# Normalizing by token halves at four stage borders of a two-block transformer kernel, with one gate product a tile moved from conv_out to gqa_out

## What is computed

```
def _modulate(t, g, shift, scale):
    return _rms(t, g) * (1 + scale) + shift
...
def _swiglu(h, w13, w2):
    gte, up = jnp.split(h @ w13, 2, axis=-1)
    return (jax.nn.silu(gte) * up) @ w2
...
        lat = lat + 0.5 * mod[:, 0, 2] * _swiglu(_modulate(lat, norm_g[i, 0], mod[:, 0, 0], mod[:, 0, 1]), ffn_w13[i, 0], ffn_w2[i, 0])
        if cx is not None:
            cx = cx + 0.5 * modc[0, 2] * _swiglu(_modulate(cx, norm_g[i, 0], modc[0, 0], modc[0, 1]), ffn_w13[i, 0], ffn_w2[i, 0])
        h = _modulate(lat, norm_g[i, 1], mod[:, 1, 0], mod[:, 1, 1])
...
        lat = lat + mod[:, 1, 2] * y
```

## Time and profile before

| | us |
|---|---|
| median of three runs | 2092.98 |
| lowest and highest of them | 2090.76 and 2093.58 |
| the profiled execution | 2093.39 |
| its span, first to last instruction | 2091.6 |

### The profile page before, as it was taken

How to read it: one execution, slowest core, us unless ns; L and a number is a source line. 1 busy time by engine, 2 the same in 40 slices (tenths; PEclk the granted TensorE clock), 3 DMA queues, 4 the chain that set the end, 5 groups by cost and what they waited for, 6 DMA issues and landing times.

```text
span 2091.6 us, 26725 instructions
## 1 busy us (share of the span) xinstructions
PE 1908.9 (91%) x10092; PEld 1624.7 (78%) x10092; DVE 1402.9 (67%) x2091; ACT 683.9 (33%) x910; POOL 126.5 (6%) x78
## 2 busy tenths in 40 slices
PE   2973799789999998998999999989999998889998
PEld 2952788778888887886788888878888887678998
DVE  7868799986666676668766666676666225856554
ACT  2443356432222213332322222232222223444432
POOL 2001300200000010002000001100000010010000
PEclk9975799889999999999999999999999999999999
DMA  9840955423443443334333344434333323223444
GB/s 377 313 168 3 238 206 188 181 93 149 150 150 125 167 175 124 134 148 151 121 143 133 146 149 159 164 121 151 141 134 118 105 94 122 91 81 141 162 163 158
DMA packets 75737, 315.77 MB, mean 151 GB/s; under 512 B 19060, under 2 KB 22904, under 8 KB 56344
## 3 DMA queue, kind: packets, MB, share of 16 engines
q1 hardware_dynamic: 75136, 314.15, 41.9%
q10 hardware_dynamic: 536, 0.79, 0.1%
HBM read 313.86 MB, written 1.06 MB: 151 GB/s over the span
## 4 chain that ended last, share of the span: by engine, by line
PE 74%; DVE 18%; ACT 3%; issue 2%; DMA 1%; POOL 1%; SPq 0%; DVEq 0%; ACTq 0%
PE acc L1294 72%; DVE Wl L810 4%; ACT Wh L526 2%; DVE tmp L797 2%; PE psN L1294 1%; DVE psGT L842 1%; DVE psGT L839 1%; DVE psGT L845 1%; DVE najunk L845 1%; DVE najunk L842 1%; DVE XT L797 1%; DMA afirst<-in_ada_w 1%; DVE small L967 1%; PE psN L1356 1%; DVE tmp L985 1%
## 5 line engine op out<-in xcount | busy, mean ns | idle before, releaser
L1294 PE MATMUL acc<-Hh,Wh 128*128 128x512 f32 (+1 forms) x2320 | 809.0, 349 | 57.1 <-DVE Hl L797 23.4
L1294 PE MATMUL acc<-Hl,Wh 128*128 128x512 f32 (+1 forms) x2320 | 801.1, 345 | 0.0
L1294 PE MATMUL acc<-Hh,Wl 128*128 128x512 f32 (+1 forms) x2320 | 800.4, 345 | 0.0
L810 DVE TENSOR_TENSOR Wl<-raw,Wh 128x2048 fp32r<-128x2048 f32 (+1 forms) x214 | 449.6, 2101 | 273.0 <-ACT Wh L526 273.0
L1294 PEld LDWEIGHTS acc<-Hh,Wh 128*128 128x128 f32 x2320 | 448.5, 193 | 119.3 <-issue 62.2
L526 ACT ACTIVATE Wh<-raw 128x2048 fp32r<-128x2048 f32 (+1 forms) x214 | 374.3, 1749 | 352.0 <-PE acc L1294 336.7
L1294 PEld LDWEIGHTS acc<-Hl,Wh 128*128 128x128 f32 x2320 | 448.7, 193 | 50.6 <-issue 0.7
L1294 PEld LDWEIGHTS acc<-Hh,Wl 128*128 128x128 f32 x2320 | 448.1, 193 | 50.7
L1294 PE MATMUL acc<-hidh,Wh 128*128 128x512 f32 (+1 forms) x704 | 259.0, 368 | 0.9 <-DVE Wl L810 0.9
L1294 PE MATMUL acc<-hidl,Wh 128*128 128x512 f32 (+1 forms) x704 | 258.6, 367 | 0.0
L1294 PE MATMUL acc<-hidh,Wl 128*128 128x512 f32 (+1 forms) x704 | 258.6, 367 | 0.0
(11 more groups left out here) (222 smaller groups left out, 1193.8 us busy)
## 6 DMA issues: line engine op xcount, KB each, us to landing
raw<-in_ffn_up SPq DMA_DIRECT2D x88, 1024.0 KB, 4.7
graw<-in_mod_w SPq DMA_DIRECT2D x144, 512.0 KB, 5.4
raw<-in_ffn_down SPq DMA_DIRECT2D x64, 704.0 KB, 4.0
graw<-in_ada_w SPq DMA_DIRECT2D x32, 512.0 KB, 6.2
raw<-in_odd_in SPq DMA_DIRECT2D x16, 1024.0 KB, 4.9
raw<-in_even_in SPq DMA_DIRECT2D x12, 1024.0 KB, 6.8
raw<-in_conv_in SPq DMA_DIRECT2D x12, 1024.0 KB, 4.7
afirst<-in_ada_w SPq DMA_DIRECT2D x8, 1024.0 KB, 13.1
```

What stands on the lines that cost most here:

```text
L810: nc.vector.tensor_tensor(Wl[:, half, 0:f], raw[:, slot, 0:f], Wh[:, half, 0:f].bitcast(f32), ALU.subtract)\
L1294: return nc.tensor.matmul(out, lhsT, rhs, start=start, stop=stop)
```

## The change

Four borders are treated by token halves: those into conv_in, ffn1_up, ffn2_up and gqa_kv (`HALVED`). At the end of the old stage the last output (the last pair of ffn_down tiles, or the last conv_out tile with its two blocks, `LAST`) is computed first for the 256 latent tokens, then for the 256 context tokens, in matmuls of 256 columns. TensorE's latent sums and the spread of the latent factors stand inside or behind the context half (`last_halved`, `lat_sums`, `lat_spreads`). The next stage begins with the latent half of its tiles 0 and 1, then the context half of both (`first_two_halved`); the context sums and spread stand behind blocks 3 and 7 of the first latent half and go to the bank psT[1], the latent ones to psN. For gqa_kv it is the latent half of the key tile, the two latent blocks of the value tile, the context half of the keys, the two context blocks of the values. VectorE does all of it in `halves_norm`, ScalarE in the new branches of `splits` and `norm`; the split of the next stage's second tile stands on both between the latent blocks and the context blocks. New semaphores lat_* carry the latent half; the context half keeps the old ones, and drained["dve"] counts one less in each of the three ffn_down stages ahead of such a border. Beside this, four tiles of gate products move from conv_out (two a tile to one) to gqa_out (none to one). The diff, cut to its core (in order: the table of stages; ScalarE's norm; VectorE's halves_norm; TensorE's first two tiles, last conv_out tile, last ffn_down pair; its program):

```diff
-    ("conv_out", 4, 16, 0, TOK, 2, "dve"),
+    ("conv_out", 4, 16, 0, TOK, 1, "dve"),
...
-    ("gqa_out", 4, 16, 0, LAT, 0, "dve"),
+    ("gqa_out", 4, 16, 0, LAT, 1, "dve"),
...
+        if name in ("ffn0_down", "ffn1_down", "ffn2_down"):
+            drained[by] -= 1
...
+        HALVED = {n: i for i, n in enumerate(["conv_in", "ffn1_up", "ffn2_up", "gqa_kv"])}
+        LAST = {n: (KC - 2, KC - 1) if n == "ffn1_up" else (KC - 1,) for n in HALVED}
...
+                if name in HALVED:
+                    for k in range(KC):
+                        act.wait_ge(lat_t, KC * HALVED[name] + k + 1)
+                        nc.scalar.activation(Hh[:, k, CL], tmp[:, k % 2, CL], ACT.Identity, bias=affine(name, k, 0)[1])\
+                            .then_inc(lat_hi, 1)
+                        if k == 2:
+                            act.wait_ge(drained["dve"], S[X_FROM[name]].drained1)
+                            for q in LAST[name]:
+                                square_half(name, q, CC)
+                    split(S[name].n0 + 1, early=True)
+                    for k in range(KC):
+                        act.wait_ge(n_t, KC * i + k + 1)
+                        nc.scalar.activation(Hh[:, k, CC], tmp[:, k % 2, CC], ACT.Identity, bias=affine(name, k, 1)[1])\
+                            .then_inc(n_hi, 1)
+                    return
...
+                dve.wait_ge(lat_done, l + 1)
+                residual_half(0, CL).then_inc(lat_res, 1)
+                meanwhile()
+                mean(0, psN, lat_ss, l + 1).then_inc(lat_mean, 1)
+                if not ffn:
+                    split(S[name].n0)
+                dve.wait_ge(lat_spread, l + 1)
+                scaled(0, 0, CL, psN).then_inc(lat_t, 1)
+                if ffn:
+                    split(S[name].n0)
+                for k in range(KC):
+                    if k + 1 < KC:
+                        if k > 0:
+                            dve.wait_ge(lat_ready, KC * l + k)
+                        scaled(k + 1, 0, CL, psN).then_inc(lat_t, 1)
+                    dve.wait_ge(lat_hi, KC * l + k + 1)
+                    low(k, 0, CL).then_inc(lat_ready, 1)
+                    if k == 2:
+                        dve.wait_ge(tile_done, s.n0 + s.tiles)
+                        residual_half(1, CC).then_inc(drained["dve"], 1)
+                    if k == 6:
+                        mean(1, psT[1], n_ss, i + 1).then_inc(n_mean, 1)
+                split(S[name].n0 + 1, early=True)
+                dve.wait_ge(n_spread, i + 1)
+                scaled(0, 1, CC, psT[1]).then_inc(n_t, 1)
+                for k in range(KC):
+                    if k + 1 < KC:
+                        if k > 0:
+                            dve.wait_ge(h_ready, H0[name] + k)
+                        scaled(k + 1, 1, CC, psT[1]).then_inc(n_t, 1)
+                    dve.wait_ge(n_hi, KC * i + k + 1)
+                    low(k, 1, CC).then_inc(h_ready, 1)
...
+                pe.wait_ge(lo_ready, s.n0 + 1)
+                pe.wait_ge(drained[s.by], s.drained0)
+                part(0, CL, lat_ready, KC * l, {3: ctx_sums, 7: ctx_spread})
+                pe.wait_ge(lo_ready, s.n0 + 2)
+                pe.wait_ge(drained["dve"], prev.drained1)
+                part(1, CL, lat_ready, KC * l, {})
+                part(0, CC, h_ready, H0[name], {}).then_inc(tile_done, 1)
+                part(1, CC, h_ready, H0[name], {}).then_inc(tile_done, 1)
...
+                    if halved(s) and isinstance(t, int) and t == s.tiles - 1:
+                        sum_of_sums(X_TO[s.name])
+                        for h, hc in enumerate((CL, CC)):
+                            for j in range(2):
+                                for k in range(KC):
+                                    last = three(acc[u % 2][h][:, j * LAT:(j + 1) * LAT], u % 2, j * KC + k, xh[:, k, hc], xl[:, k, hc],
+                                                 k == 0, k == KC - 1)
+                                if h == 1 and j == 0:
+                                    lat_sums(X_TO[s.name])
+                            last.then_inc((lat_done, tile_done)[h], 1)
+                        lat_spreads(X_TO[s.name])
+                        return
...
+                    part(0, 0, CL)
+                    sum_of_sums(name)
+                    part(0, 1, CL).then_inc(lat_done, 1)
+                    part(1, 0, CC, lat_sums).then_inc(tile_done, 1)
+                    lat_spreads(name)
+                    part(1, 1, CC).then_inc(tile_done, 1)
...
             ffn_down(S["ffn0_down"])
-            norm("conv_in")
             linear(S["conv_in"])
             linear(S["conv_out"], xh=cyh, xl=cyl)
-            norm("ffn1_up")
             linear(S["ffn1_up"])
```

More of the change, by code:

```diff
@@ L212, in build @@
         c_tanh = sem("c_tanh")
+        lat_done, lat_res, lat_sq, lat_ss, lat_mean, lat_rstd, lat_spread, lat_t, lat_hi, lat_ready = (
+            sem("lat_" + x) for x in ("done", "res", "sq", "ss", "mean", "rstd", "spread", "t", "hi", "ready"))
         nmx = small[:, 0:64]
@@ L905, in step @@
                 def step(t, u, i):
+                    if halved(s) and t == s.tiles - 1:
+                        modulation_of(s, t, u, i)
+                        return
                     next_split(s, t, u, i)
@@ new lines, in ctx_sums, with ctx_spread @@
+            def ctx_sums(name):
+                pe.wait_ge(n_sq, KC * NORMS[name] + KC)
+                for q in LAST[name]:
+                    for b in range(2):
+                        ins = nc.tensor.matmul(psT[1][:, b:b + 1], tmp[:, q % 2, (2 + b) * P:(3 + b) * P], ones[:, 0:1],
+                                               start=False, stop=q == KC - 1, skip_group_check=True)
+                ins.then_inc(n_ss, 1)
+            def ctx_spread(name):
+                pe.wait_ge(n_rstd, NORMS[name] + 1)
+                for b in range(2):
+                    ins = spread(psT[1][:, b * P:(b + 1) * P], rstd, 2 + b)
+                ins.then_inc(n_spread, 1)
@@ L1361, in sum_of_sums @@
                 pe.wait_ge(n_sum, SUM0[name] + SUMMED[name])
+                if name in HALVED:
+                    for h, bank in enumerate((psN, psT[1])):
+                        for b in range(2):
+                            nc.tensor.matmul(bank[:, b:b + 1], tmp[:, 2, (2 * h + b) * P:(2 * h + b + 1) * P], ones[:, 0:1],
+                                             start=b == 0, stop=False, skip_group_check=True)
+                    return
                 sum_of(name, tmp[:, 2, :], True, False)
```

117 lines of the change are left out of this document (108 added, 9 removed).

## The result

The changed kernel takes **2099.42 us** (median of 9 runs, 2097.94 to 2101.36), the kernel before 2093.24 (median of 9, 2090.76 to 2094.44): a ratio of 1.0032, with a 95% interval of 1.0024 to 1.0040. It is 6 us slower. The prediction was 2096.0, range 2089 to 2103: the time is in the range, but above the bound of 2097.2 under which I had called it no change, so the outcome is one to which I had given 0.37. The profiled execution took 2101.36, 8.0 above that of before.

The account below looks back on a forecast made before the run. TensorE is busy 91% of the span; winnable is its idle or low-clock time at stage borders. -2.3 - 0.9 - 2.4 + 5.2 + 3.5 = +3.1 on 2093.39 gives 2096.5, as median 2096.0, range 2089 to 2103.

Parts of the forecast that it names:

- The border into conv_in: Into conv_in: with halves and a high clock, tile 1 done at 823.8 instead of 826.1, a gain of 2.3 us.
- Four stands of the sum: At conv_in, TensorE waits: 0.5 before the sum of sums, 1.1 before block 0, 0.9 for the context residual, 2.5 before tile 1.
- rival (a): Clock also falls in short stands at conv_in, gqa_kv, ffn2_up: 2.4 us each, +7, 2103; chance 0.20.
- ffn2_up and gqa_kv: Borders into these stages: gain 0.9 us at ffn2_up (2.3 less 1.4), gain 2.4 at gqa_kv (2.3 + 0.7 less 0.6).
- The border into ffn1_up: From conv_out: TensorE stands 7.2 us before the last tile, the clock falls; a loss of 5.2 us.
- My bound for a clock that holds: At the border from conv_out into ffn1_up: the loss is 2.1 us if the clock stays up.
- gqa_out: In gqa_out: added product pairs and slower GpSimd adds make the last residual 3.5 us late, a loss of 3.5.
- the 5.5 us at half clock: Behind the old border into conv_in: matmuls ran 5.5 us at 1.2 GHz, counted as a cost.
- (b): At conv_out: TensorE is not held at the sum of sums, all borders gain as designed, 2088 to 2085; chance 0.07.
- (c): Clock held at conv_out (2.1) and the products at gqa_out swallowed, 2089.5; chance 0.10.
- (d): Splitting matmuls into 256 columns costs almost nothing, 2091.4, a border gain of 1 to 1.5 each; chance 0.08.
- my 13: Splitting a 512-column matmul into two of 256 columns costs 13 ns a pair, from 0.120 against 0.227 us.

Follow-up runs that it names:

- before again: The kernel before, unchanged, profiled a second time; 2094.04 us.
- products_only: The kernel before with only the table of stages changed: one pair of gate products a tile in conv_out and in gqa_out; 2091.87 us, ratio 0.9997.
- products_ffn2: The kernel before with four of conv_out's eight pairs of gate products moved into ffn2_down's first four tiles, none in gqa_out; 2088.50 us, ratio 0.9983.
- halves_and_ffn2: The changed kernel with the sum of sums directly ahead of the latent sums, and four product pairs in ffn2_down's first tiles, none in gqa_out; 2086.02 us, ratio 0.9966.
- experiment 4: The run conv_out_busy: the changed kernel with 25 unread matmuls in the stand before the last conv_out tile; 2095.86 us, ratio 1.0016.
- conv_out_busy: The changed kernel with 25 matmuls nobody reads put into TensorE's stand before the last conv_out tile; 2095.86 us, ratio 1.0016.
- three_borders: The changed kernel with ffn1_up's border and the gate products as before, halves only into conv_in, ffn2_up and gqa_kv; 2091.47 us, ratio 0.9992.
- products_back: The changed kernel with the gate products back: two pairs a tile in conv_out, none in gqa_out; 2097.88 us, ratio 1.0024.
- before_kept_busy: The kernel before with unread matmuls in the three stands of each norm; 2092.23 us, ratio 0.9997.
- halves_kept_busy2: halves_and_ffn2 with unread matmuls filling TensorE's stands at the borders, the fewer-matmul version in ffn3_up's norm; 2083.45 us, ratio 0.9955.
- sum_late: The changed kernel with the sum of sums moved from the head of the last conv_out tile to directly ahead of the latent sums; 2089.47 us, ratio 0.9984.

## Why the prediction was right or wrong, step by step

**The border into conv_in: steps right, clock wrong.** Four stands of the sum were met within 0.12 us, and tile 1 was done at 824.2 against a forecast of 823.8. The profile of the changed kernel shows the gain of 2.3 (2.5), but it is the rarer case: in its second profile, and in six of seven with this border halved and its stand empty, the clock fell behind the stand of 2.4 us, and 1.0 is left. That is rival (a). It names the right mechanism at a price of 2.4 where 1.5 was measured here and at gqa_kv, and the fall comes and goes from one execution to the next, which neither the forecast nor the rival had as a possibility.

**ffn2_up and gqa_kv.** 0.8 and 0.2 against a forecast of 0.9 for ffn2_up, and 1.4 and 2.9 against 2.4 for gqa_kv. But other profiles of the kernel before (before again, products_only, products_ffn2) are themselves 0.9 to 1.0 faster at gqa_kv than the one I measured against; against those the halves bring 0.5 or 2.0.

At ffn2_up the sum held that lost time is free for TensorE as long as it would only wait for tile 1's weights. The runs bear this out, for the clock too. Tile 1's first matmul in halves_and_ffn2, where the clock stays up, and in the changed kernel, where it is at half from 1371.6 on; then the second profile of the changed kernel, where the half clock lasts longer:

```profile
1370.22 0.39 PE L1411 MATMUL acc<-Hh,Wh 128*128 128x256 f32 x1 [1.69 <-DVE Wl L865]
...
1379.32 0.38 PE L1410 MATMUL acc<-Hh,Wh 128*128 128x256 f32 x1 [0.21 <-DVE Wl L864]
...
1370.20:1376.60 6.40, 5.34 (x26) 5.37 (x26) 4.46 (x11) 3.93 (x7) 0.00 (x0) 0.50 0.55 225
```

The wait shrinks from 1.69 to 0.21 us and the column is -0.8 in both. With the longer stretch no wait is left before tile 1 and the gain is 0.2. So a fall costs 0 to 0.6 us here, where rival (a) had 2.4.

**The border into ffn1_up: right, 5.0 and 4.4 against 5.2.** The stand before the last tile (6.3 for 7.2), its releaser, the clock's fall in it and the 4.29 before ffn1_up (in the sum: 4.7 from the stage's end to the first matmul) are as described. Inside the sum the clock was too small: 3.4 and not 2.7 (experiment 4), the stand itself too large. My bound for a clock that holds, 2.1, does not follow from my own terms (5.2 less 2.7 and 1.0 is 1.5). Experiment 4 lost 1.6, but there the clock fell once more behind the last tile, so no run tests this bound as such.

**gqa_out: the products right, what stands around them left out.** The last residual came 3.4 late (20.66 less 17.27) against 3.5; products_only, with the same products, lost 3.4 in all. (The pair is 2.8 us by its own rows, 788.53 to 791.33, and not 2.7.) But the end of the kernel is 4.8 and 5.0 late. The sum was closed at the last residual, and the traces show what it left out:

- A fall of the clock at the end of the attention delays the first residual of gqa_out as well, by 0.5 and 0.7 us in the two profiles. Of the thirteen profiles against the first of before, the six with such a fall lose 0.1 to 0.7 there, the seven without lose nothing.
- From the last residual to the first matmul of ffn3_up it takes 7.4 us in each kernel whose stands are empty. But the half clock behind the last residual reaches a different way into the first tile of ffn3_up. Its 48 matmuls take 7.2 us in before, 7.6 and 7.8 in the two profiles of the changed kernel, and 8.5 in conv_out_busy and three_borders. The half clock in that tile, in before, after and conv_out_busy:

```profile
1886.00:1889.00 3.00, 2.97 (x14) 3.00 (x15) 2.89 (x7) 1.53 (x3) 0.00 (x0) 0.50 0.85 339
...
1893.10:1897.30 4.20, 4.19 (x20) 4.20 (x20) 4.06 (x10) 2.17 (x5) 0.00 (x0) 0.50 0.51 215
...
1886.70:1892.70 6.00, 6.00 (x28) 6.00 (x29) 5.60 (x13) 3.05 (x6) 0.00 (x0) 0.50 0.37 154
```

- Another 0.3 to 0.4 us are lost at the beginning of ffn3_down, some 65 us before the end. The cause is open.

With the 3.4 these make 4.8 (0.5, 0.5, 0.4) and 5.0 (0.7, 0.6, 0.3). The kernels three_borders and products_back have no products there: the 1.3 of the one is the second item alone, the 1.6 of the other is 0.7, 0.6 and 0.3 (this last later in ffn3_down).

**The sum.** Forecast +3.1 on the profiled execution; measured +8.0 and +6.2, in the medians +6.2. Over the forecast the second profile has 1.3 at conv_in (clock), 0.7 at ffn2_up, 1.5 at gqa_out and ffn3, 0.8 in the attention, and under it 0.8 at conv_out and 0.5 at gqa_kv: 3.0. The 1.3 at conv_in is the clock, as are the 0.7 at ffn2_up and all but 0.3 of the 1.5 at the end; the attention's 0.8 goes with a fall of the clock too, and falls there come without the change. So the steps hold, and what is missing in the sum is half clock at places where it had kept the clock up or had not looked. That the time is in the range at all is in part luck: the forecast alone ended at 2099, and the 2103 was the end of rival (a), whose three falls at 2.4 us each did not come in that form.

**A statement of the prediction that fell.** It counted the 5.5 us at half clock behind the old border as a cost of the kernel before, and so as something that halves could save. before_kept_busy shows 0.7 for it. The sum did not use it, since each border was worked out to an end time; the reading of the profile was wrong all the same.

**The rivals.** (b), not held at the sum: refuted by the stand of 6.30. (c), clock held and products swallowed: neither. (d), the split almost free: 144 matmuls of 256 columns follow one another in 17.54 us (1005.20 to 1024.10 less its 1.36), 0.122 each, so a pair costs 17 ns over a full one of 0.227, more than my 13. (My 6.1 us in all took conv_out's 48 at 7 ns; at 13 it is 6.4.) The estimate by the rule of the Trainium skill (TensorE: Matmul & The Clock Gate, "Wait — 56ns, not 53.3ns?"), 2.5 ns a pair, does not hold here.

**What the change was worth.** Halving four borders brings 2.5 us (halves_and_ffn2 against products_ffn2), products at the right place 4.3, filling the stands behind halves another 1.9 to 2.6. The version with all three, halves_kept_busy2, takes 2083.45: 0.9955 of before. The change lost because one line, the sum of sums, stood at the head of a tile for which its operands could not be ready; without that stand it is 3 us faster than before (sum_late), although the products at gqa_out still cost it 3.4.
